# Regrouping the expert blocks of a mixture-of-experts stage, finishing its last block by halves, and splitting the next block's first weights ahead of its norm

## The reference

```python
h = modulate(rms_norm(x, mixer_norm_g[l]), sh1, sc1)
proj = h @ w_in[l]                       # 1024 -> 3584
...
x = x + g1 * (mixed @ w_out[l])
h2 = modulate(rms_norm(x, ffn_norm_g[l]), sh2, sc2)
x = x + g2 * hierarchical_moe(h2, ...)
x = rms_norm(x, final_norm_g)

def hierarchical_moe(h, ...):            # 32 experts, each token goes to TOP_K = 2 of one group of 8
    ...
    act = silu(einsum("td,edh->teh", t, w_g)) * einsum("td,edh->teh", t, w_u)
    out = einsum("teh,ehd->td", act * combine[:, :, None], w_d)

h = layer_norm(ALPHA * h + token_mixer(h, ...))   # 12 weight tiles of projections, 4 of output
h = layer_norm(ALPHA * h + peer_ffn(h, ...))      # queries, top-k over 16384 experts, dense u and v
```

## Time and profile before

| what | value |
|---|---|
| median of 3 runs | 3073.71 us (3071.75 to 3073.74) |
| profiled execution | 3071.7 us |
| its span, first to last instruction | 3070.1 us |
| PE busy | 2924.7 us (95%), 17633 matmuls |
| DVE busy | 1732.7 us (56%) |
| ACT busy | 1258.3 us (41%) |
| DMA, mean over the span | 203 GB/s, 622.20 MB |
| granted TensorE clock, mean | 0.974 |
| expert stage, layer one: first gate-up to last down's start | 251.27 to 509.16 us |
| expert stage, layer two: the same | 740.75 to 999.25 us |

### The profile page before, as it was taken

The page is one execution under the profiler, slowest core; times in us unless marked ns, Lnnn a source line. Parts: engine busy times, 40 slices in busy tenths (PEclk is TensorE's granted clock), DMA queues, the critical chain, the costliest instruction groups (busy, mean ns, idle before and its releaser), DMA issues.

```text
span 3070.1 us, 50902 instructions
## 1 busy us (share of the span) xinstructions
PE 2924.7 (95%) x17633; PEld 2355.5 (77%) x17633; DVE 1732.7 (56%) x3503; ACT 1258.3 (41%) x2144; POOL 34.2 (1%) x73
## 2 busy tenths in 40 slices
PE   7989998998999898999999999989899999999998
PEld 4774434785434778999999888878799999978886
DVE  3533212634212464997898555555479969955555
ACT  1131102122111454444676444445444467644444
POOL 0000000000000100000000000020000000000000
PEclk9999999998999999999999999999999999999999
DMA  9727988734998323454433555543345443345553
GB/s 392 279 80 327 414 331 342 283 128 198 382 393 356 140 79 142 171 184 169 148 125 134 183 190 185 185 153 110 112 168 183 181 151 125 137 164 191 183 186 123
DMA packets 85797, 622.20 MB, mean 203 GB/s; under 512 B 9664, under 2 KB 9664, under 8 KB 10112
## 3 DMA queue, kind: packets, MB, share of 16 engines
q1 hardware_dynamic: 84816, 616.61, 52.6%
q10 hardware_dynamic: 576, 2.65, 0.2%
q0 software_dynamic: 240, 0.82, 0.1%
HBM read 618.99 MB, written 1.05 MB: 202 GB/s over the span
## 4 chain that ended last, share of the span: by engine, by line
PE 86%; DVE 4%; DMA 4%; ACT 2%; issue 2%; DVEq 1%; SPq 0%; ACTq 0%
PE acc L622 25%; PE lin L622 20%; PE duo L622 9%; PE lin L808 7%; PE lin L584 6%; PE duo L838 4%; PE acc L1072 4%; DMA arena<-w_moe 2%; PE duo L584 2%; PE acc L852 2%; DMA ada_home<-w_moe 1%; PE acc L658 1%; DVE w_lo L1515 1%; PE lin L725 1%; DMA arena<-w_ada 1%
## 5 line engine op out<-in xcount | busy, mean ns | idle before, releaser
L1123 ACT ACTIVATE w_hi<-slot 128x1024 fp32r<-128x1024 f32 x608 | 642.4, 1058 | 580.1 <-PE acc L622 388.2
L1515 DVE TENSOR_TENSOR w_lo<-slot,w_hi 128x1024 fp32r<-128x1024 f32 x608 | 741.6, 1221 | 186.7 <-ACT w_hi L1123 174.6
L622 PE MATMUL acc<-w_hi,x_parts 128*128 128x512 f32 x2176 | 554.4, 397 | 3.3 <-ACT w_hi L1123 3.3
L622 PEld LDWEIGHTS acc<-w_hi,x_parts 128*128 128x128 f32 x2176 | 409.4, 188 | 103.1 <-ACT w_hi L1123 3.7
L622 PE MATMUL lin<-x_parts,w_hi 128*128 128x256 f32 x3392 | 457.1, 287 | 17.3 <-DVEq L1848 11.0
L622 PEld LDWEIGHTS lin<-x_parts,w_hi 128*128 128x128 f32 x3392 | 429.3, 192 | 20.1 <-issue 16.1
L622 PE MATMUL acc<-w_lo,x_parts 128*128 128x512 f32 x1088 | 299.0, 396 | 0.0
L1512 DVE TENSOR_TENSOR x_parts<-arena,x_parts 128x256 fp32r<-128x256 f32 x256 | 108.9, 425 | 321.1 <-ACT x_parts L1128 321.1
L622 PEld LDWEIGHTS acc<-w_lo,x_parts 128*128 128x128 f32 x1088 | 204.9, 188 | 50.0
L622 PE MATMUL lin<-x_parts,w_lo 128*128 128x256 f32 x1696 | 240.3, 284 | 0.8
L622 PE MATMUL duo<-x_parts,w_hi 128*128 128x256 f32 x1728 | 231.0, 286 | 4.2 <-ACT w_hi L1123 4.2
(11 more groups left out here) (350 smaller groups left out, 3066.5 us busy)
## 6 DMA issues: line engine op xcount, KB each, us to landing
slot<-wstream SPq DMA_DIRECT2D x348, 1024.0 KB, 4.8
arena<-w_moe SPq DMA_DIRECT2D x136, 1024.0 KB, 15.4
arena<-w_ada SPq DMA_DIRECT2D x28, 1024.0 KB, 9.0
slot<-w_moe SPq DMA_DIRECT2D x28, 1024.0 KB, 17.6
ada_home<-w_moe SPq DMA_DIRECT2D x28, 1024.0 KB, 15.5
ada_home<-w_ada SPq DMA_DIRECT2D x20, 1024.0 KB, 7.9
xT<-x_in ACTq DMA_DIRECT2D x1, 1024.0 KB, 5.5
out<-xT ACTq DMA_DIRECT2D x1, 1024.0 KB, 3.9
```

What stands on the lines that cost most here:

```text
L622: return mm(out_, a, b, start=start, stop=stop)
L1123: last = A(w_hi[c % 2][:, :], slot[j % SLOTS][:, (c % 2) * HALF:(c % 2 + 1) * HALF], ACT.Copy)
L1515: TT(w_lo[c % 2][:, :], slot[j % SLOTS][:, (c % 2) * HALF:(c % 2 + 1) * HALF], w_hi[c % 2][:, :].bitcast(F32), ALU.subtract).then_inc(slot ...
```

## The change

Four things.

1. `BLOCKS` is put into another order, and its block 12 of three groups, (6: 64), (6: 32), (5: 32), becomes four groups of 32, three of them rank 6. `windows_of` merges groups of one rank again for the window copies and for `expect`.
2. The last block (p = 17) is finished by halves: `down` signals after its first bank, `y_high` and `y_low` work on 512 columns each, `spread` starts on its first four chunks after the first half and closes each bank of `acc` as soon as its two chunks are in; DVE's additions wait bank by bank.
3. `root_table`: ACT makes a dummy Sqrt of one column ahead of the squares of both norms of a layer.
4. ACT's first two and DVE's first weight part of block two are made ahead of the norm in front of it: the first `high_part` ahead of the squares, the second behind the root, `low_part` behind DVE's additions. At the end of each layer of block two the parts of the next layer's first tile are made ahead of the layer norm (for the last layer with one extra 1 MB load). Between the blocks the gain is now multiplied in by DVE, ACT makes all of x_hi first and xT behind it, and DVE's three constants are made ahead of its additions.

The semaphore counts follow (`Y_PARTS`, `spread_done` and `moe_done` of each bank).

```diff
-BLOCKS = [((0, 0, 128),), ((0, 128, 128),), ((9, 0, 64), (10, 0, 64)), ((11, 0, 64), (12, 0, 64)),
-          ((15, 0, 32), (16, 0, 32), (17, 0, 32), (18, 0, 32)), ((1, 0, 128),), ((1, 128, 128),),
-          ((7, 0, 64), (8, 0, 64)), ((13, 0, 64), (14, 0, 64)),
-          ((23, 0, 32), (24, 0, 32), (25, 0, 32), (26, 0, 32)), ((2, 0, 128),), ((2, 128, 64), (5, 0, 64)),
-          ((6, 0, 64), (6, 64, 32), (5, 64, 32)), ((31, 0, 32),),
-          ((27, 0, 32), (28, 0, 32), (29, 0, 32), (30, 0, 32)), ((4, 0, 128),), ((3, 0, 128),),
-          ((19, 0, 32), (20, 0, 32), (21, 0, 32), (22, 0, 32))]
+BLOCKS = [((3, 0, 128),),
+          ((13, 0, 64), (14, 0, 64),),
+          ((4, 0, 128),),
+          ((31, 0, 32),),
+          ((7, 0, 64), (8, 0, 64),),
+          ((19, 0, 32), (20, 0, 32), (21, 0, 32), (22, 0, 32),),
+          ((1, 0, 128),),
+          ((1, 128, 128),),
+          ((11, 0, 64), (12, 0, 64),),
+          ((23, 0, 32), (24, 0, 32), (25, 0, 32), (26, 0, 32),),
+          ((2, 0, 128),),
+          ((2, 128, 64), (5, 0, 64),),
+          ((6, 0, 32), (6, 32, 32), (6, 64, 32), (5, 64, 32),),
+          ((27, 0, 32), (28, 0, 32), (29, 0, 32), (30, 0, 32),),
+          ((0, 0, 128),),
+          ((0, 128, 128),),
+          ((9, 0, 64), (10, 0, 64),),
+          ((15, 0, 32), (16, 0, 32), (17, 0, 32), (18, 0, 32),)]
...
+                        if p == MOE_BLOCKS - 1 and n == KC // 2:
+                            pe.wait_ge(y_lo_ready, l * Y_PARTS + p + 2)
...
+                        if p == MOE_BLOCKS - 1 and n % 2 == 1:
+                            mm(acc[:, n // 2, :], zeros[:, :], zero_row, start=False, stop=True).then_inc(moe_done, 1)
...
+                        for n in range(2):
+                            act.wait_ge(y_done, l * Y_PARTS + p + 1 + n)
+                            A(Y_HI[:, n * 512:(n + 1) * 512], duo[:, n, :], ACT.Identity,
+                              scale=slot_w[:, p % 2:p % 2 + 1]).then_inc(y_hi_ready, 1)
...
                 y_high(MOE_BLOCKS - 1)
+                root_table()
+                if l + 1 == L:
+                    high_part(L * (TILES1 // SLOTS), 0, 0, 0)
                 for n in range(KC):
                     act.wait_ge(x_added, l * ADDS1 + OUT_T + n + 1)
                     square(n)
                 root(l * 4 + 5, D)

+            high_part(L * (TILES1 // SLOTS), 1, 0, 0)
             for k in range(KC):
                 act.wait_ge(scaled_x, L * 2 * KC + k + 1)
-                g = par(cst, COLC, "final_g")[:, k:k + 1]
-                last = A(x_hi[:, k, :], H[:, k], ACT.Identity, scale=g)
+                last = A(x_hi[:, k, :], H[:, k], ACT.Copy)
                 if k % 2 == 1:
                     last.then_inc(x_hi_ready, 1)
-                A(xT[:, k, :], H[:, k], ACT.Identity, scale=g).then_inc(x_chunks, 1)
+            for k in range(KC):
+                A(xT[:, k, :], H[:, k], ACT.Copy).then_inc(x_chunks, 1)
...
+                for c in range(2):
+                    high_part(rings + TILES2 // SLOTS, c, 0, pairs + 2 * U_T)
                 ln_normalized(1, "ln2_g", "ln2_b")
...
-                dve.wait_ge(moe_done, l + 1)
+                else:
+                    TS(ALPHA_I, ident[:, :], ALPHA, None, ALU.mult)
+                    TT(later[:, :], later[:, :], ident[:, :], ALU.add)
+                    V.memset(EPS_COL, EPS2)
+                    dve.drain().then_inc(alpha_made, 1)
                 for n in range(KC):
+                    if n % 2 == 0:
+                        dve.wait_ge(moe_done, l * 4 + n // 2 + 1)
                     STT(xT[:, n], accT[:, n, :], mod[:, 5 * KC + n:5 * KC + n + 1], xT[:, n],
                         ALU.mult, ALU.add).then_inc(x_added, 1)
+                if l + 1 == L:
+                    low_part(0, 0, 0)
                 dve.drain().then_inc(layer_end1, 1)
...
             rstd(L * 3 + 1)
+            fg = par(cst, COLC, "final_g")
+            for k in range(KC):
+                STT(H[:, k], xT[:, k], fg[:, k:k + 1], RSTD[:, 0], ALU.mult, ALU.mult).then_inc(scaled_x, 1)
+            for k in range(KC):
+                dve.wait_ge(x_hi_ready, k // 2 + 1)
+                last = TT(x_lo[:, k, :], H[:, k], x_hi[:, k, :].bitcast(F32), ALU.subtract)
...
+                low_part(0, 0, number + 4 * U_T)
                 ln_statistics(l * 2 + 2, root0 + 2)
...
+            def root_table():
+
+                A(lamb[:, 11:12], ones[:, 0:1], ACT.Sqrt)
```

More of the change, by code:

```diff
@@ L97 @@
     assert _at >= min(T, TOP * T // (_r + 1))
-FAR = ((128, 0, 3), (64, 5, 7))
+FAR = ((128, 0, 3), (64, 5, 6))
 EXPERT_AT = NE + sum(b - a for _, a, b in FAR)
@@ L113, in rows_of, with windows_of @@
         at += n
+    return out
+def windows_of(b):
+    out = []
+    for rank, start, rows in rows_of(b):
+        if out and out[-1][0] == rank:
+            out[-1] = (rank, out[-1][1], slice(out[-1][2].start, rows.stop))
+        else:
+            out.append((rank, start, rows))
     return out
@@ L839, in down @@
                                           start=(k == 0), stop=(k == 1))
+                                if p == MOE_BLOCKS - 1 and (n, k, i) == (0, 1, final):
+                                    last.then_inc(y_done, 1)
                                 if n == 1 and k == 1 and set_free(p, i, 2) and i != final:
@@ L1773, in _ @@
                 for c, block in enumerate(BLOCKS):
-                    for rank, _, rows in rows_of(c):
+                    for rank, _, rows in windows_of(c):
                         V.tensor_copy(expect[rows, c:c + 1], number[rows, rank:rank + 1])
@@ L1783, in window @@
                     V.memset(lamb[:, 8:9], 0.0)
-                    pieces = [(PLACE_AT[rank, start], rows) for rank, start, rows in rows_of(p)]
+                    pieces = [(PLACE_AT[rank, start], rows) for rank, start, rows in windows_of(p)]
                     at = [dve.value_load(table[0:1, a:a + 1], min_val=0, max_val=2 * T) for a, _ in pieces]
@@ L1891, in _ @@
                 number = l * (2 * PAIRS2)
-                for c in range(2 * QK_T + 1):
+                for c in range(1, 2 * QK_T + 1):
                     low_part(c, c // 2, number)
```

53 lines of the change are left out of this document (27 added, 26 removed).

## The result

The changed kernel takes 3017.8 us (median of four runs, 3016.04 to 3019.43) where the kernel before took 3072.7 (3070.11 to 3073.74, four runs): 0.9819 of it, with a 95% interval of 0.9806 to 0.9833. The profiled executions took 3071.7 and 3019.1 us, with spans of 3070.1 and 3017.5 us, so the traces are 52.6 us apart where the medians are 54.9. The prediction was 3024.5 us, with a range of 3015 to 3038.5.

The account below looks back on a forecast made before the run. PE carries most of the chain, with DMA nearly equal in the expert stage (239 us each). Terms 34.0 + 9.2 + 1.1 + 3.0 + 1.9 = 49.2 us off 3071.7 give 3022.5, plus 2.0 for the median: 3024.5 us, range 3015 to 3038.5.

Parts of the forecast that it names:

- The bound and the surplus: Expert stage: PE and DMA limits both 239 us; mixed-width block 12 costs PE 13.3 us extra per layer.
- the other way in which the prediction could have failed: Expert stage: the prediction fails if the clock falls where PE is now busy; no size given.
- The stage: Expert stage, block 12 in one width plus new order: 17.0 us saved per layer, 34.0 in all.
- the end that I had put at 19: Expert stage: upper end of the saving per layer, 19 us if waits nearly all go.
- The tail: Last block's down to last addition, finished by halves and banks: 4.6 us saved per layer, 9.2 in all.
- The root table: Norms of both layers, square-root table loaded ahead of the squares: 0.27 us four times, 1.1 in all.
- Block two's start: First weight parts ahead of the norm and a shorter way to x_lo: 3.0 us saved, ends 1.5 and 4.5.
- the change of layer: Inside block two, next layer's first weight parts made ahead of the layer norm: 1.9 us saved.
- the end at 0: Change of layer in block two: no gain if PE, like DVE, stands without work at the loop end.
- DMA takes the place: Rival, expert stage: 7 of the 17 us per layer turn into waits for tiles, 3038.5 us; chance 0.14.
- Full or partial issue in turn: Rivals, block 12: groups sharing a tile issue at 0.33 us each (about 3058, chance 0.04) or 0.43 (3085, chance 0.03).
- More than forecast: Rival, expert stage and tails: all waits go and tails give 5.5 us, about 3016 us; chance 0.07.

Follow-up runs that it names:

- half_tiles: The changed kernel, loading only half of each expert tile from the 14th of a layer on (output not the reference's): 3007.7 us, one run.
- parts_late: The changed kernel with block two's first weight parts made where they were before, the new x_hi order kept: 3014.9 us.
- halved_late: two_halved with DVE's small work (next layer's modulation, three constants) behind its eight additions: 3015.9 us.
- no_halves: The changed kernel with the last block whole, one closing of the four banks at the end and one wait of DVE: 3025.1 us.
- no_root_table: The changed kernel without the dummy root ahead of the squares: 3017.8 us.
- two_halved: The changed kernel with its last two blocks finished by halves instead of only the last: 3014.3 us.

## Why the prediction was right, and where it was off

**The bound and the surplus.** Right. Block 12 costs 7.08 and some 3.6 us; width alone gives 13.1 us in layer one, for 13.3 worked out from the earlier trace rows, and 10.7 in layer two, where more went into a wait for tiles. That three groups read one tile, which no row of before showed, costs nothing. The clock stayed at 1.00 in both stages, the other way in which the prediction could have failed.

**The stage, 34.0 us forecast, 38.2 measured.** The mechanism was right and the size too low. The failed step is how I took the difference: 17.3 us between two sets of steps, 507.7 and 490.4, cut to 17.0. The steps of the new order were good (last down at 490.4 for the 490.6 of the trace; a stage of 239.1 us for 238.6 and 239.6); those of the old one were 1.5 and 2.0 us too short against the earlier trace rows. Against the trace's 257.9 the same steps give 18.8 a layer, where 19.3 and 18.9 came. That is the end that I had put at 19 for waits that nearly all go, yet not all went: PE's weight loads wait 8.5 us for w_moe in each stage of before, and 2.9 and 3.9 us in the changed ones, which lie 3.3 and some 4.1 above PE alone. That the steps of the new order came out so near is in part luck: 236.4 us of PE and 2.7 of waits stand there for 235.2 and 3.3.

**The tail, 9.2 forecast, 7.2 in the table and 7.3 as the runs with and without have it.** The steps behind a full-speed down were right: 9.15 us to the last addition, and half_tiles, where nothing waits for tiles, has 8.9 in both layers. The term was mis-sized in its bases. I subtracted from 13.75, in which down was 4.79 us long, and gave the new tail a down of 3.64; but the changed kernel's last down is 4.72 and 5.29 us long, since it now waits for its last tiles. So a gain of the stage was partly paid here: the two terms are not independent, and their sum, 45.4 us for 43.2, is nearer than either. The repetition of the changed kernel says the same: its stages were 240.6 and 238.9 us, which is 36.9 less than before, and from the last down to the last addition it took 9.77 and 9.24 us, which is 8.6 less. The split moved by more than 1 us, the sum is 45.5. In the total (52.6 us between the traces, 49.2 forecast) the stage's 4.2 us too little and the tail's 2.0 too much partly cancel.

**The root table, 1.1.** Its mechanism stands by the traces (0.5 at a mid norm, 0.2 at the first end), with some 0.3 us against it at block two's start, where I had put 0.1. No run can show the sum.

**Block two's start, 3.0, and the change of layer, 1.9.** 3.2 and 2.55 measured. Half of the first is the parts: 15.46 for 13.73 with and without them; the rest the shorter way from the norm to x_lo. At the change of layer I feared the loop's end. The Trainium skill, Runtime: NRT & Kernel Launch, section Instruction fetch mechanics, has a taken branch to a target outside the fetched window stall. ACT (2.31 us) and DVE (3.34) do stand idle at it in parts_late, waiting for nothing that the profile shows; that it is the fetch is not shown. PE starts 0.39 us after it fell idle (the row at 1992.40), and 0.80 and 0.85 us in halved_late and no_halves, and PE is what counts once its operands are made before the branch. So the end at 0 was wrong. That the gain went beyond 1.9 is the clock and luck. no_halves, half_tiles and halved_late, whose code there is the same, have 3.6 us, which is the forecast's 3.64; in the changed kernel eight of the matmuls behind x_lo took 1.52 us for 2.07 in the query projection of before, because the granted clock was 0.73 over them, for 0.50.

**What I had not counted.** The first, fourth, eighth and tenth stretch of the table give 1.4 us, the root's mid-norm share among them. Between the kernels whose block two is the same code (the changed one, its repetition, no_root_table, no_halves, two_halved, halved_late, half_tiles) these layers vary by 2.8 and 2.3 us, 1013.3 to 1016.1 and 1016.5 to 1018.8. What the table shows there is of that size, and I don't read it as an effect.

**The rivals.** DMA takes the place: the run with half of the tiles' bytes leaves 3.3 and some 4.1 us a layer for waits on tiles, not 7 more than I had. Full or partial issue in turn, the two rivals on the shared tile: refuted by the 7.08 us. More than forecast (3016) was nearest to what came, though its number did not follow from its terms: 19 us a layer and tails of 5.5 add up to 3018.7. The measured 3017.8 lies 0.2 us below the forecast's own range of 3018 to 3032.

## What to carry to other kernels

When matmuls are packed on column groups, give all groups of a block one width, if need be by cutting one group into several that read the same moving tile: that was free here, while unequal widths did not overlap at all. When two resources are nearly balanced, a slow spot of one is a hole in the other, so anchor the forecast at the traced waits and not at the difference of two models; and expect the last consumer of the stage to inherit what is left. A part worth 4 us, in a kernel whose clock falls in gaps, needs its own stretch read in the trace and two pairs of kernels with and without it: one pair alone showed the wrong sign, inside the noise.

## What the runs showed of the hardware that I had not expected

- Column groups of 64 and 32 never ran beside each other: a matmul of the other width started 0.52 us later, one of the same width on other columns 0.01 us later. Each change of width cost 0.13 us above the 0.43 of a lone matmul (15.88 and 14.27 us, with 12 changes fewer).
- Three groups may take one tile as moving data at no cost: 64 matmuls in 7.08 us, the same as with four tiles (7.08 us for the block at 448.45 of before, in the same kind of view).
- The same code met the TensorE clock at 0.66 or at 0.83 over a stretch of 20 us, in kernels that differ only in the expert stage and so in when the stretch begins. The second layer of block two took 1019.7 and 1016.0 us in these two (both with the parts late).
